# Column tiles of 32 in a delta-rule inverse, a rebuilt start and end, and halves of projection pieces between the inverse's rounds

## The reference, cut to what matters

```python
def gated_delta_rule(q, k, v, g, beta):     # chunks of 64 here, of 104 in the kernel
    ...
    decay = jnp.exp(jnp.where(incl, g[..., :, None] - g[..., None, :], -jnp.inf))
    lower = jnp.where(strict, jnp.einsum('bhnid,bhnjd->bhnij', kb, k) * decay, 0.0)
    sol = lax.linalg.triangular_solve(lower + eye, rhs, left_side=True, lower=True, unit_diagonal=True)
...
h = h + hierarchical_moe(rms_norm(h, ffn_norm_w), ...)     # for expert e: (silu(x @ w_gate[e]) * (x @ w_up[e])) @ w_down[e]
out = rms_norm(h, final_norm_w)
```

## Time and profile before

| what | value |
|---|---|
| three executions | 1317.53, 1320.84, 1321.98 us; median 1320.84 |
| the profiled execution | 1320.21 us |
| its span, first to last instruction | 1318.4 us |
| mean granted clock of TensorE | 0.984 of full |
| busy: PE, DVE, ACT, POOL | 1271.6, 895.0, 723.4, 173.4 us |

### The profile page before, as it was taken

One profiled execution on the slowest core, in us unless ns is written; L12 is line 12 of the kernel. 1 busy time (PEld: TensorE's weight loads), 2 busy tenths in 40 slices (PEclk: granted clock), 3 DMA queues, 4 the chain that ended last, 5 costly groups with the idle time before them and its releaser, 6 DMA issues.

```text
span 1318.4 us, 20659 instructions
## 1 busy us (share of the span) xinstructions
PE 1271.6 (96%) x8344; PEld 1102.9 (84%) x8344; DVE 895.0 (68%) x1060; ACT 723.4 (55%) x919; POOL 173.4 (13%) x144
## 2 busy tenths in 40 slices
PE   6999999999999999999988999999999999999977
PEld 5989999999999999778877888888888888888854
DVE  6744556455644573434457989888988989898846
ACT  7351335133603351524235887878888888788733
POOL 0020111011102110600011111111111111011100
PEclk9989999999999999999988999999999999999989
DMA  7100000000010100245417999999999999999886
GB/s 210 49 16 33 18 33 33 33 18 32 33 34 17 49 18 14 115 161 207 166 59 264 384 374 382 381 388 397 395 386 394 385 385 383 384 390 381 324 330 247
DMA packets 38053, 273.66 MB, mean 208 GB/s; under 512 B 8147, under 2 KB 8403, under 8 KB 25700
## 3 DMA queue, kind: packets, MB, share of 16 engines
q1 hardware_dynamic: 28340, 251.67, 50.0%
q0 software_dynamic: 9216, 16.80, 3.3%
q10 hardware_dynamic: 432, 4.27, 0.8%
HBM read 260.11 MB, written 29.36 MB: 220 GB/s over the span
## 4 chain that ended last, share of the span: by engine, by line
PE 85%; DVE 6%; DMA 3%; ACT 3%; issue 1%; SPq 0%; DVEq 0%; POOLq 0%; ACTq 0%
PE bank L590 12%; PE bank L592 12%; PE bank L591 12%; PE bank L1292 8%; PE bank L1294 8%; PE bank L1293 8%; DMA w_raw<-in_w_up 2%; PE bank L481 2%; PE bank L477 2%; PE bank L479 2%; PE bank L581 2%; PE bank L1424 2%; PE bank L1427 2%; DVE arena L1830 1%; PE bank L1408 1%
## 5 line engine op out<-in xcount | busy, mean ns | idle before, releaser
L955 DVE TENSOR_TENSOR w_lo<-w_raw,w_hi 128x2048 fp32r<-128x2048 f32 x192 | 432.6, 2286 | 35.6 <-ACT w_hi L736 35.2
L736 ACT ACTIVATE w_hi<-w_raw 128x2048 fp32r<-128x2048 f32 x192 | 360.8, 1917 | 67.9 <-DMA w_raw<-in_w_up 46.0
L1292 PE MATMUL bank<-xn_hi,p_hi 128*128 128x364 f32 (+1 forms) x672 | 230.1, 342 | 2.1 <-DVE p_lo L1765 2.1
L1294 PE MATMUL bank<-xn_hi,p_lo 128*128 128x364 f32 (+1 forms) x672 | 216.9, 323 | 0.0
L1293 PE MATMUL bank<-xn_lo,p_hi 128*128 128x364 f32 (+1 forms) x672 | 216.5, 322 | 0.0
L590 PE MATMUL bank<-w_hi,xgT_hi 128*128 128x512 f32 x512 | 206.5, 403 | 2.9 <-DVE xgT_lo L1013 2.9
L592 PE MATMUL bank<-w_hi,xgT_lo 128*128 128x512 f32 x512 | 201.4, 393 | 0.0
L591 PE MATMUL bank<-w_lo,xgT_hi 128*128 128x512 f32 x512 | 200.9, 392 | 0.0
L1292 PEld LDWEIGHTS bank<-xn_hi,p_hi 128*128 128x128 f32 x672 | 127.8, 190 | 4.7 <-DVE p_lo L1765 2.5
L1293 PEld LDWEIGHTS bank<-xn_lo,p_hi 128*128 128x128 f32 x672 | 128.0, 190 | 0.3
L1294 PEld LDWEIGHTS bank<-xn_hi,p_lo 128*128 128x128 f32 x672 | 127.5, 190 | 0.0
(11 more groups left out here) (259 smaller groups left out, 1942.4 us busy)
## 6 DMA issues: line engine op xcount, KB each, us to landing
w_raw<-in_w_down SPq DMA_DIRECT2D x32, 2048.0 KB, 10.0
w_raw<-in_w_gate SPq DMA_DIRECT2D x31, 2048.0 KB, 10.9
w_raw<-in_w_up SPq DMA_DIRECT2D x31, 2048.0 KB
p_raw<-in_w_tiles SPq DMA_DIRECT2D x28, 512.0 KB, 3.2
arena<-y_rows SPq DMA_DIRECT2D x8, 1024.0 KB, 14.2
arena<-in_tokens SPq DMA_DIRECT2D x10, 416.0 KB
w_out_raw<-in_w_out SPq DMA_DIRECT2D x4, 1024.0 KB, 9.4
arena<-in_tokens SPq DMA_DIRECT2D x8, 512.0 KB, 4.4
```

The source lines that it names most:

```text
L736: nc.scalar.activation(w_hi[m][:, half], wraw[m][:, half], ACT.Copy).then_inc(hi_done[m], 1)
L955: nc.vector.tensor_tensor(w_lo[m][:, half], wraw[m][:, half], w_hi[m][:, half].bitcast(F32), ALU.subtract).then_inc(lo_done[m], 1)
L1292: nc.tensor.matmul(out[:, 0:n], p_hi[slot][:, k, :], hi, start=(k == 0), stop=False)
L1294: m = nc.tensor.matmul(out[:, 0:n], p_lo[slot][:, k, :], hi, start=False, stop=(k == KD - 1))
```

## The change

Six things are changed together.

1. **Inverse.** The diagonal blocks of levels 1 to 4 are now 32 wide (32, 32, 32 and 8 in a chunk) instead of 64 and 40. The transpositions `ttr1` to `ttr4` become products with the identity on the same blocks. Level 5 takes two off-diagonal corners per chunk with 32 output rows each, and level 6 splits its 64 output rows into two products of 32. DVE's part of level 5 becomes two small instructions per group instead of one.
2. **Fills.** In heads 0 to 2, the pieces UU 1, UU 2, GB 0 and GB 1 are issued in halves of 12 matmuls, spread behind `ttr1`, `ttr2`, `ttr3` and the `z` and `rz` rounds of levels 2 to 4.
3. **Beginning.** The third chunk's transposes go to banks 7 and 2 and wait for nothing but their input; the fourth chunk's transposes move behind the first projection piece. ACT and DVE orders are rewritten to match.
4. **End, loads.** The residual rows of blocks 0 to 6 are loaded during the last expert: 0 to 3 ahead of its down weights, 4 to 6 behind them.
5. **End, sums.** For blocks 0 to 4 DVE adds the whole first result (1024 columns instead of 512), and PE drops line 667's product. The last block is scaled and stored in two halves.
6. **Spare loop.** The loop for overfull experts uses one weight buffer; it runs for no expert in these executions. The last expert's up split on DVE is spread around another instruction.

```diff
-            for t in range(4):
-                residual_rows(t)
+            refill(E - 1, 1, E - 1)
+            residual_rows(0)
+            refill(E - 1, 2, E - 1)
+            residual_rows(1)
...
+                if t >= WHOLE:
+                    nc.tensor.matmul(pair_of[1], ident, yf[t][:, 512:D], start=False, stop=False)
...
-                tt(hf[t][:, 0:512], hf[t][:, 0:512], yf[t][:, 0:512], ALU.add).then_inc(f_sum, 1)
+                w = D if t < WHOLE else 512
+                tt(hf[t][:, 0:w], hf[t][:, 0:w], yf[t][:, 0:w], ALU.add).then_inc(f_sum, 1)
...
-        BLOCKS = (slice(0, HALF), slice(HALF, C))
+        BLOCKS = [slice(b, min(b + 32, C)) for b in range(0, C, 32)]
+        PAIR_Z = f"z{LEVELS - 2}"
+        CORNERS = [(BLOCKS[0], BLOCKS[1]), (BLOCKS[2], BLOCKS[3])]
+        FULL_TURNS = ("ttr0", f"ttr{LEVELS - 2}")
...
+        def turn_bank(t, b):
+            return bank[(7, 2)[b] if t == 2 else 3 + 2 * (t % 2) + b]
...
-                for t in ((3,), (4,), (5, 6), (7,), (8,), (9,))[n] if n < 6 else ():
+                for t in ((), (3, 4), (5, 6), (7,), (8,), (9,))[n] if n < 6 else ():
...
+                        elif name in FULL_TURNS:
+                            m = nc.tensor.transpose(o, rT[0:C, c, :], ident[0:C, 0:C])
                         elif name.startswith("ttr"):
-                            m = nc.tensor.transpose(o, rT[0:C, c, :], ident[0:C, 0:C])
+                            for b in BLOCKS:
+                                m = nc.tensor.matmul(o[b, b], rT[0:C, c, b], ident[0:C, b], start=True, stop=True)
                         elif name == LAST_Z:
-                            m = nc.tensor.matmul(o[0:HALF, HALF:C], lM[HALF:C, c, 0:HALF], rT[HALF:C, c, HALF:C], ...)
+                            for b in BLOCKS[0:2]:
+                                m = nc.tensor.matmul(o[b, HALF:C], lM[HALF:C, c, b], rT[HALF:C, c, HALF:C], ...)
+                        elif name == PAIR_Z:
+                            for b, q in CORNERS:
+                                m = nc.tensor.matmul(o[b, q], lM[0:C, c, b], rT[0:C, c, q], start=True, stop=True)
...
-                    fills = {"z1": [(GC, 2)], "rz1": [(UU, 0)], "z2": [(UU, 1)], "rz2": [(UU, 2)], "z3": [(GB, 0)],
-                             "rz3": [(GB, 1)], "rz4": [(GB, 2)]}
+                    fills = {"z1": [(GC, 2)], "rz1": [(UU, 0)], "ttr1": [(UU, 1, LOW)], "z2": [(UU, 1, HIGH)],
+                             "rz2": [(UU, 2, LOW)], "ttr2": [(UU, 2, HIGH)], "z3": [(GB, 0, LOW)], "rz3": [(GB, 0, HIGH)],
+                             "ttr3": [(GB, 1, LOW)], "z4": [(GB, 1, HIGH)], "rz4": [(GB, 2)]}
...
+                    elif name == PAIR_Z:
+                        for b, q in CORNERS:
+                            m = nc.vector.tensor_copy(zz[b, s, q], bmat(g)[b, :, q])
```

More of the change, by code:

```diff
@@ L727, in tail_scalar, with split @@
                     rows_turned(4)
-            def split(e, m, halves=(0, 1)):
+            def split(e, m, halves=(0, 1), raw=None):
                 act.wait_ge(w_sem[m], e * 16 + 16)
@@ L735, in split @@
                     half = slice(b * WU // 2, (b + 1) * WU // 2)
-                    nc.scalar.activation(w_hi[m][:, half], wraw[m][:, half], ACT.Copy).then_inc(hi_done[m], 1)
+                    nc.scalar.activation(w_hi[m][:, half], wraw[m if raw is None else raw][:, half], ACT.Copy).then_inc(hi_done[m], 1)
             act.wait_ge(r_dve, GRP_DIFF)
@@ L1131, in tail_vector @@
                 if t + 3 < FT:
-                    first_half(t + 3)
-            scaled(FT - 1)
+                    first_row(t + 3)
+            dve.wait_ge(f_rstd, FT)
+            for b in range(2):
+                cols = slice(b * 512, (b + 1) * 512)
+                stt(of[FT - 1][:, cols], hf[FT - 1][:, cols], stat[:, (FT - 1) % 2, 2:3], fw[:, cols], ALU.mult,
+                    ALU.mult).then_inc(f_out, 1)
         def tail_pool(pool):
@@ L1504, in mixer @@
                         rnd(h, name)
-                        for kind, pc in fills.get(name, ()):
-                            fill(h, kind, pc)
+                        for part in fills.get(name, ()):
+                            fill(h, *part)
                     if n < LEVELS - 1:
                         rnd(h, f"ttr{n}")
+                        for part in fills.get(f"ttr{n}", ()):
+                            fill(h, *part)
                     if n == 5:
@@ L1789, in _ @@
                 token_scale(t)
-            for t in range(NC):
-                xn_low(t)
-                if t == 0:
-                    lo_part(1, 1)
-                if t == 2:
-                    token_scale(3)
-                    lo_part(2, 1)
-                if t >= 2 and t + 2 < NC:
-                    token_scale(t + 2)
-                if t == 3:
-                    lo_part(0, 1)
+            xn_low(0)
+            xn_low(1)
+            lo_part(1, 1)
+            xn_low(2)
+            token_scale(3)
+            lo_part(2, 1)
+            for t in range(4, 7):
+                token_scale(t)
+            xn_low(3)
+            xn_low(4)
+            lo_part(0, 1)
+            token_scale(7)
+            xn_low(5)
+            xn_low(6)
+            token_scale(8)
+            token_scale(9)
+            for t in range(7, NC):
+                xn_low(t)
             dve.wait_ge(wab_done, 1)
```

118 lines of the change are left out of this document (72 added, 46 removed).

## The result

The changed kernel takes 1309.98 us (median of 19 executions, 1305.95 to 1317.64), the kernel before in the same rounds 1320.05 us. The ratio is 0.9931, 95% interval 0.9916 to 0.9947: about 10 us less, where 22.6 were forecast. That lies in the wide range (1292 to 1316) and outside the forecast's own (1293 to 1301). It is also where rival A stood, but by luck: A's reason, slower rounds, did not happen. The profiled execution is the fastest of the 19, 1305.95 us with a span of 1304.1, so the two traces differ by 14.3 us in span.

What follows compares the result with a forecast made beforehand. PE was taken to bound the kernel, busy for 1271.6 of 1318.4 us. The terms 13.4 + 2.7 + 2.1 + 0 + 4.4 = 22.6 us off 1320.2 gave a forecast of 1297.5 us, range 1292 to 1316, its own 1293 to 1301.

Steps and rivals of the forecast that it cites:

- rival A: Inverse: small records don't run four abreast, a round takes 1.0 to 1.4 us; mostly 1308 to 1317 us, chance 0.17.
- s = 0.75 us a round: Inverse: the time over which a round's 80 records start, with four 32-column tiles side by side; lower bound 0.63.
- rival B: Inverse: issue at 29.7 ns a record bounds each round, 2.37 us a round; slower, about 1377 us, chance 0.10.
- Heads, 13.4 us: Inverse of heads 0 to 2: shorter rounds take 4.45 us off each head, 13.4 us in three.
- So the halves earn nothing by themselves: Fills of heads 0 to 2: half pieces only cover ACT's and DVE's evacuations and keep shorter rounds from waiting; 0 us.
- the last head, -2.7 us: Inverse of the last head: levels 1 and 2 gain 1.6 and 0.1 us, levels 3 and 4 0, levels 5 and 6 1.0.
- Beginning, 2.1: Beginning: PE's unbroken stretch starts at 16.3 instead of 18.40 us, 2.1 us off, bounds 0 and 3.3.
- Beginning and end, 6.5: Both ends: 2.1 us off at the beginning, 0 from the end's loads and 4.4 from its sums.
- Rival C: Only the inverse gains; both ends give 0 to 2 us instead of 6.5, so 1302 to 1305 us; chance 0.11.
- The inverse as a whole, 16.1 us: Inverse of all four heads: 13.4 us off in heads 0 to 2 and 2.7 in the last.
- seven places: Fills: the places where halves must cover evacuations; if that fails, each costs at most 1.37 us.

Runs made afterwards that it cites:

- after_again: The changed kernel run once more with no edit, beside the kernel before: 1310.4 us, ratio 0.9908.
- twice_last: The changed kernel with each 32-column product of `z3`, `rz3`, `z4` and `rz4` of the last head issued twice: 1314.54 us in one execution.
- wout_late: The changed kernel with the `w_out` load started only after level 4 of the last head: 1312.95 us in one execution.
- last_wide: The changed kernel with levels 3 to 6 of the last head as before the change: 1300.48 us, ratio 0.9825 to the kernel before.
- start_only: The kernel before with only the rebuilt beginning: ratio 0.9982 to the kernel before.
- whole_fills: last_wide with whole projection pieces and the earlier DVE order in heads 0 to 2: 1309.56 us, ratio 0.9912 to the kernel before.

## Why the prediction was wrong

- **s = 0.75 us a round: right.** 0.71 measured, four tiles abreast. Rivals A and B fell.
- **Heads, 13.4 us: 11.0 in the trace, 7.2 in that of after_again.** In head 1 of the first trace a `z` or `rz` round gives PE back after 0.84 us instead of 1.31, 3.8 us in all, more than the 3.3 forecast. Level 6 gave its 0.6, level 5 only 0.1 instead of 0.35: DVE's six small instructions took 1.42 us where 1.37 stood before and 1.2 were expected. Tiled transposes with halves behind them gave 0.9, the seams of the halves took 1.1 back, and the stop for instructions in `rz3` took another 0.5. With whole transposes three heads give 13.1.
- **"So the halves earn nothing by themselves": true only on wide products (0.3 us a head).** With narrow ones they are what feeds PE: a half is 24 instructions for 2 us. At 14 ns, a round and a half need 184 x 14 = 2.6 us of supply for 3.0 us of work, which just holds, by this estimate. I had them cover only evacuations.
- **The failed step: the last head, -2.7 us, "In levels 3 and 4 DVE has convolution and splitting besides, and PE waits for it [...]; shorter rounds only wait longer, 0".** It was +7.7: 8.4 us of stops for instructions and 17 us at half clock, against rounds that were 0.47 us shorter. The step put the shorter rounds at nothing; it had no term for the instructions that they need. The shown causes are the rate (twice_last), the load that slows it (wout_late), each from one execution, and the form of these levels (last_wide, 10 us back). Two levels have 480 records, 960 instructions; at 14 ns that is an estimated 13.4 us of supply for some 6 us of work. My rival B had priced issue as a limit on every round, for which 29.7 ns at the earlier trace rows stood; here it is a limit on the mean over some 256 instructions, and shows only where nothing long dilutes them.
- **Beginning, 2.1:** 2.4 by the ratio of start_only, with an interval from nothing to 4.8. The first projection matmul came at 16.7 to 16.9 instead of 16.3, and in five traces PE goes on behind the convolutions 0.7 to 1.5 us earlier, so part of the 2.4 may be the clock's, and that the number is met is in part luck. **Beginning and end, 6.5:** 6.7. The early residual rows cost nothing that shows. Rival C fell.
- **The inverse as a whole, 16.1 us:** the change is at 0.9931 and the two ends alone at 0.9949, so the rebuilt inverse and the halves gave about 2 us, which these intervals don't tell from nothing.
- **Slips that change little:** the eight halves were counted as seven places, round `rz2` of the last head has one piece behind it and not two, and the first projection piece before the change starts at 19.74, not 20.05, since the 1.65 us of the earlier trace rows hold the whole last record.

With the failed step mended (last_wide) the kernel takes 1300.5 us, ratio 0.9825, where the forecast was 1297.5 or 0.9823. Its parts by the traces are less than the whole: heads 11.4, last head 1.3 and both ends 6.7 make 19 of some 23 us, and the rest isn't located.

Open: why the clock between 70 and 84 us is full in some executions of one order and not in others; how much of the last head's loss the half clock alone is, since no run had stops of this length without it; and whether a block's time is a round trip or a bandwidth.

## What to carry to other kernels

Count instructions per microsecond, not only array time, when products are made smaller: a form that is faster between long matmuls can be slower on a bare stretch, and the same table must not serve both. Small work and long work belong alternately in the stream; where a stretch has none of the long, take fewer, larger instructions. A stop in mid-round with "issue" as its releaser, repeating after a fixed number of records, is the mark of it. "issue" alone isn't: both traces also have it for 5.5 us ahead of the end's first identity product.

## What the runs showed that I had not expected

- In the starved stretches instructions came in blocks of 256 (16 KB), one per 3.5 to 4.0 us, and one per 6.2 while the DMA engines carried some 390 to 430 GB/s. PE emptied a block at 9 ns a record with its load.
- Four column tiles of 32 run at 9 ns from record to record, each with its own weight load.
- Behind the first stops of the last head the clock fell to its lower level and stayed there for 17 us, in the other three traces with such stops for 20, 24 and 31. In head 1 of whole_fills the slower clock cost more than the stop itself. Not every fall has a stop ahead of it: the dips in heads 0 to 2 of after_again don't.
